# Making the low parts of the weights on VectorE instead of GpSimd in a decoder-layer kernel

## The reference

```python
h = rmsnorm(x, norm_pre_mix) * (1.0 + sc_m) + sh_m
proj = h @ w_in
(hq, hf, hi, hg, aq, ak, av, iq, ik, iw) = jnp.split(proj, split_points, axis=-1)
o_hg = hgrn2_mixer(hq, hf, hi, hg, ...)
o_att = dsa_mixer(aq, ak, av, iq, ik, iw, positions, ...)
y = jnp.concatenate([o_hg, o_att], axis=-1) @ w_out
x = x + gt_m * rmsnorm(y, norm_post_mix)
h = rmsnorm(x, norm_pre_ffn) * (1.0 + sc_f) + sh_f
gate, up = jnp.split(h @ w_ffn_in, 2, axis=-1)          # 1024 -> 2 x 2816
y = (jax.nn.silu(gate) * up) @ w_ffn_out                # 2816 -> 1024
x = x + gt_f * rmsnorm(y, norm_post_ffn)
```

## Time and profile before

| | us |
|---|---|
| median of 3 runs | 853.19 (852.34 to 853.39) |
| the profiled execution | 851.23 |
| its span | 849.4 |
| TensorE busy in it | 771.6 (91%) |
| VectorE / ScalarE / GpSimd busy | 326.3 / 284.0 / 278.2 |

### The profile page before, as it was taken

The page is one execution under the profiler, slowest core; times in us unless marked ns, Lnnn a source line. Parts: engine busy times, 40 slices in busy tenths (PEclk is TensorE's granted clock), DMA queues, the critical chain, the costliest instruction groups (busy, mean ns, idle before and its releaser), DMA issues.

```text
span 849.4 us, 10172 instructions
## 1 busy us (share of the span) xinstructions
PE 771.6 (91%) x3530; PEld 591.9 (70%) x3530; DVE 326.3 (38%) x651; ACT 284.0 (33%) x458; POOL 278.2 (33%) x156
## 2 busy tenths in 40 slices
PE   3697988999999887998997999999999996999996
PEld 2175655777776656665686788888888885888885
DVE  1198237969697762432405500000000003222214
ACT  4153344242423233324326522222222222122222
POOL 1154220313132122115540444444444445344430
PEclk9689899999999998998999899999999998999999
...
DMA packets 100594, 87.99 MB, mean 104 GB/s; under 512 B 3828, under 2 KB 89944, under 8 KB 99544
## 3 DMA queue, kind: packets, MB, share of 16 engines
...
...
## 4 chain that ended last, share of the span: by engine, by line
PE 76%; DVE 13%; issue 5%; ACT 2%; DMA 2%; SPq 1%; DVEq 0%; POOL 0%; ACTq 0%; POOLq 0%
PE ps L1131 43%; PE ps L1150 19%; PE ps L1307 2%; PE ps L1188 2%; DMA w_raw<-in_w_in 2%; DVE score L901 1%; DVE score L937 1%; PE ps L1375 1%; DVE act L966 1%; DVE top L932 1%; PE ps L1370 1%; PE ps L1350 1%; PE ps L1184 1%; PE ps L1434 1%; DVE h_lo L815 1%
## 5 line engine op out<-in xcount | busy, mean ns | idle before, releaser
L402 POOL TENSOR_TENSOR w_lo<-w_raw,w_hi 128x1024 fp32r<-128x1024 f32 (+1 forms) x107 | 255.6, 2399 | 532.9 <-ACT w_hi L461 532.9
L1131 PE MATMUL ps<-h_hi,w_hi 128*128 128x512 f32 x616 | 253.9, 412 | 9.1 <-DVE h_lo L815 6.5
L1131 PE MATMUL ps<-h_lo,w_hi 128*128 128x512 f32 x616 | 243.6, 395 | 0.0
L1131 PE MATMUL ps<-h_hi,w_lo 128*128 128x512 f32 x616 | 243.6, 395 | 0.0
L1131 PEld LDWEIGHTS ps<-h_hi,w_hi 128*128 128x128 f32 x616 | 117.6, 191 | 51.6 <-issue 18.4
L461 ACT ACTIVATE w_hi<-w_raw 128x1024 fp32r<-128x1024 f32 (+1 forms) x107 | 110.0, 1050 | 125.7 <-PE ps L1150 99.7
L1131 PEld LDWEIGHTS ps<-h_hi,w_lo 128*128 128x128 f32 x616 | 117.4, 191 | 26.2
L1131 PEld LDWEIGHTS ps<-h_lo,w_hi 128*128 128x128 f32 x616 | 117.8, 191 | 23.9 <-issue 1.2
L1150 PE MATMUL ps<-w_hi,h_hi 128*128 128x512 f32 x240 | 95.1, 396 | 7.2 <-DVE h_lo L1106 6.4
L1097 DVE TENSOR_TENSOR act<-adaw,ps 128x512 f32 x22 | 15.1, 688 | 221.9 <-PE ps L1131 221.9
L1150 PE MATMUL ps<-w_lo,h_hi 128*128 128x512 f32 x240 | 94.3, 393 | 0.0
...
## 6 DMA issues: line engine op xcount, KB each, us to landing
...
```

The costliest lines, as they stand in the source:

```text
L402: pool.tensor_tensor(w_lo[slot][:, 0:n], w_raw[slot][:, 0:n], w_hi[slot][:, 0:n].bitcast(f32), ALU.subtract).then_inc(lo_ok, 1)
L1131: last = mm(ps[bank][0:rows, :], a, b, start=(k == 0 and n == 0), stop=(k == KT - 1 and n == 2))
```

## The change

From group 25 on (the key projection of head 1) the low parts of the weights are made by VectorE: 82 of the 107 splits, and all eight `split_x_lo`. GpSimd ends after group 24. The splits are put into VectorE's order by hand: in a head one behind the ropes, one before the fourth reduction and one behind the last `normalise`; in the last head the activation splits ahead of the ropes and, with a weight split each, behind the first and second `normalise`; in FFN-in two before each of a pass's multiplications; in FFN-out one behind each `split_act`.

In the last FFN-in group TensorE now counts `h_free` after each of its first four steps, and VectorE splits `act` into slots 0 to 3 as they come free. TensorE starts FFN-out with row tiles 0, 2 and 3 of the first group and takes tile 1, whose banks hold the last multiplication's input, when `act_ok[1]` says so. The last pass of FFN-in is written out behind the loops of TensorE and VectorE.

```diff
@@ gpsimd
             with pool.Fori(0, HG_HEADS) as h:
                 stage_hg(h)
-            with pool.Fori(0, ATT_HEADS) as h:
-                stage_att(h)
...
-            with pool.Fori(0, FT // 2) as i:
-                for u in range(4):
-                    split_lo(i * 4 + (G_FIN + u), u)
-            with pool.Fori(0, FT // 4) as i:
-                for u in range(4):
-                    split_lo(i * 4 + (G_FOUT + u), u)
...
+            split_lo(G_ATT + 2, 2)
+            split_lo(G_ATT + 3, 0)
@@ vector
+            def split_lo(g, slot, n=1024):
+                ve.wait_ge(hi_ok, g + 1)
+                V.tensor_tensor(w_lo[slot][:, 0:n], w_raw[slot][:, 0:n], w_hi[slot][:, 0:n].bitcast(f32),
+                                ALU.subtract).then_inc(lo_ok, 1)
+            def split_x_lo(k):
+                ve.wait_ge(xs_hi, k + 1)
+                part_k = slice(k * SEQ, (k + 1) * SEQ)
+                V.tensor_tensor(h_lo[:, part_k], mix[:, part_k], h_hi[:, part_k].bitcast(f32),
+                                ALU.subtract).then_inc(xs_ok, 1)
...
             def att_body(h, first, last):
                 rot = slice(0, 32)
                 for n, dst in enumerate((aq, ak)):
+                    if last:
+                        split_x_lo(n)
                     ve.wait_ge(a_swap, h * 2 + (n + 1))
...
+                split_lo(h * 3 + (G_ATT + 4), 1)
                 if first:
                     head_tail(HG_HEADS - 1)
...
                     if t:
                         normalise(t - 1)
+                    if last and t in (1, 2):
+                        split_x_lo(t + 1)
+                        split_lo(G_OUT + 1 + t, 1 + t)
+                    elif not last and t == 2:
+                        split_lo(h * 3 + (G_ATT + 5), 2)
                 normalise(TT - 1)
+                if not last:
+                    split_lo(h * 3 + (G_ATT + 6), 0)
                 adaln_set(h)
...
+            for k in range(4, KT):
+                split_x_lo(k)
+            for k in range(4, KT):
+                split_lo(G_OUT + k, k % 4)
             ve.wait_ge(x_again, 16 * TT)
...
             ve.wait_ge(scale_ok, 2)
+            split_lo(G_FIN, 0)
             norm_features(1, 24, scale_ffn)
-            with ve.Fori(0, FT // 2) as i:
+            split_lo(G_FIN + 1, 1)
...
+            with ve.Fori(0, FT // 2 - 1) as i:
                 for v in range(2):
+                    for u in (2 * v + 2, 2 * v + 3):
+                        split_lo(i * 4 + (G_FIN + u), u % 4)
+                    swiglu(i, v)
...
             def split_act(k, slot):
                 at = slice(slot * SEQ, (slot + 1) * SEQ)
-                ve.wait_ge(group_done, k + (G_FOUT - 3))
+                if isinstance(k, int) and k < 4:
+                    ve.wait_ge(h_free, k + 1)
+                else:
+                    ve.wait_ge(group_done, k + (G_FOUT - 3))
...
+            for u in (2, 3):
+                split_lo(G_FOUT - 4 + u, u)
+            swiglu(FT // 2 - 1, 0)
+            ve.wait_ge(act_ok[0], 2)
+            ve.wait_ge(act_ok[1], 2)
+            split_lo(G_FOUT, 0)
+            for u in range(3):
+                split_act(u, u)
+            swiglu(FT // 2 - 1, 1)
+            split_lo(G_FOUT + 1, 1)
+            split_act(3, 3)
+            split_lo(G_FOUT + 2, 2)
+            split_lo(G_FOUT + 3, 3)
             for v in range(2):
                 ve.wait_ge(act_ok[v], FT // 2)
-            ve.wait_ge(group_done, G_FOUT)
-            with ve.Fori(0, FT // 4) as i:
+            with ve.Fori(1, FT // 4) as i:
                 for u in range(4):
                     split_act(i * 4 + u, u)
+                    split_lo(i * 4 + (G_FOUT + u), u)
@@ tensor
                 if k == KT - 1:
                     last.then_inc(group_done, 1)
+                elif freeing:
+                    last.then_inc(h_free, 1)
...
-            with te.Fori(1, FT // 2) as i:
+            with te.Fori(1, FT // 2 - 1) as i:
                 fin_pass(i, False)
-            for v in range(2):
-                te.wait_ge(act_ok[v], FT // 2)
-            for k in range(4):
-                row_group(G_FOUT + k, k, k, KT + k + 1, k == 0)
+            fin_pass(FT // 2 - 1, False, True)
+            te.wait_ge(lo_ok, G_FOUT + 1)
+            te.wait_ge(xs_ok, KT + 1)
+            te.wait_ge(act_ok[0], FT // 2)
+            for t in (0, 2, 3, 1):
+                if t == 1:
+                    te.wait_ge(act_ok[1], FT // 2)
+                last = row_tile(0, 0, t, True)
+            last.then_inc(group_done, 1)
+            for k in range(1, 4):
+                row_group(G_FOUT + k, k, k, KT + k + 1)
```

43 lines of the change are left out of this document (14 added, 29 removed).

## The result

The changed kernel takes 840.33 us, median of four runs (839.40 to 840.88), against 852.77 us (851.62 to 853.39, four runs) for the kernel before: a ratio of 0.9855, 95% interval 0.9838 to 0.9872. The profiled execution took 840.83 us, with a span of 838.9.

The account below looks back on a forecast made before the run. TensorE, busy 91% of the span, bounds the kernel, so only its waits can earn: -7.75 - 2.0 + 0.5 - 1.63 + 1.04 + 0.85 = -9.0 us, from 851.23 to 842.2, plus 2 for the median: 844.2 us, range 841.0 to 848.0.

Parts of the forecast that it names:

- Price of a split: VectorE's cost for one moved 128x1024 weight split: 1.25 us, extrapolated from 256 and 512 columns; bounds 0.75 and 2.4.
- rival (c): Moved splits cost VectorE the same 2.4 us as GpSimd: +8.7 us, 852.9 us, no change; chance 0.04.
- Step to FFN-out: From FFN-in to FFN-out: TensorE's 6.42 us gap and 1.33 us lost at half clock both go, -7.75 us.
- Rival (b): Handover to FFN-out only half covered: TensorE idles up to 2 us, half clock stays, 847.5 us; chance 0.1.
- Start of FFN-in: First FFN-in groups: subtractions no longer stretched by GpSimd, -2.0 us, between 1.3 (clock still drops) and 2.6.
- rival (a): Kinder clock: no half clock in the first head and at FFN-in, -1.3 and -0.6, 842.3 us; chance 0.2.
- Head 0 and the gates: First attention head +0.5 us, including +1.3 for half clock; gates behind it -1.63 us as their split moves.
- Heads 1 and 2: Split between ropes and first logits reduction delays TensorE's fourth logits by 0.52 us per head: +1.04 us.
- Last head: Activation split ahead of first rope delays the partner matmul; fillers wait 0.6 + 0.5 us for splits: about +0.85 us.
- The step that failed: From the forecast profiled execution, 842.2 us, to the median: 2 us added as before, giving 844.2 us.
- (d): FFN-in, pair of splits behind the third group: above 2.5 us each VectorE's queue delays TensorE, +16, 860 us; chance 0.03.
- (e): Change fails to do what it says, if TensorE frees no slot before its last matmul; counted under Rival (b).

Follow-up runs that it names:

- r1: Changed kernel with all its moved splits but the old step from FFN-in to FFN-out, without the slot-by-slot splitting: 845.84 us, ratio 0.9937.
- r2: Kernel before with only the slot-by-slot splitting and new row tile order; GpSimd still makes all low parts: 848.95 us, ratio 0.9969.
- r4: The changed kernel timed again, same code, in five rounds against the kernel before: 840.97 us, ratio 0.9883.
- r3: Changed kernel, but GpSimd keeps the splits up to the output projection (groups 0 to 40, eight activation splits): 841.59 us, ratio 0.9893.

## Why the prediction was short in its time, and how its terms fared

- **Price of a split**, 1.25 us: 1.22 measured. The extrapolation from half the size held; rival (c), 2.4 us on VectorE as on GpSimd, falls. The Trainium skill, "Perfetto Trace Analysis", section "Optimizing Scalar/DVE Operations", warns that offloading between GpSimd and VectorE might not help; here it did, with 1.22 us in place of 2.4 and no row of the FFN stretched any more. The prediction's 2.00 us beside a split, against 0.41, is this row of the kernel before:

```profile
284.91 2.00 DVE L964 TENSOR_TENSOR act<-act 128x256 f32<-128x256 f32 x1
```

- **Step to FFN-out**, -7.75: -7.97. The room everywhere was there, and r1 and r2 show that it needed both parts. Rival (b) did not occur: VectorE began slot 0 at 708.75 and TensorE never waited.
- **Start of FFN-in**, -2.0: -2.46. Mis-sized: I took the half clock to stay in part; it went altogether, in this as in r4's trace. The bound of 2.6 was the better value. That is the half of rival (a) that came true.
- **Head 0 and the gates**, -1.13: -1.03 in the first pair of traces, -1.6 on average. The first agreement is two misses that cancel: head 0 cost 0.97 where 0.5 was said, the gates gave 2.00 where 1.63 was. The wait of 2.4 us ahead of the third logits is 2.69. The gates' gap fell by 1.62 as said, and the products behind it took 5.44 us instead of 5.81, a gain that was put at nothing. The half clock in head 0 was put at +1.3 us as if it were certain. In six traces it was absent once, lasted 3.3 us four times (1.6 us lost against the trace without it) and 6.9 us once (3.0 us lost).
- **Heads 1 and 2**, +1.04: +0.67, 0.33 each instead of 0.52.
- **Last head**, +0.85: +1.44, +1.3 on average. One part of the mechanism was right: the partner matmul waits behind the activation split, 0.74 us longer where 0.6 was said. The other was wrong: the 0.6 + 0.5 us of idle charged for fillers that wait behind the queued splits came out at 0 in this trace and 0.3 in two others, and the wait of 0.79 us ahead of the logits went. TensorE idles no longer than before; the whole +1.44 is half clock, 10.0 us of it in this trace against 6.6 before, for which the forecast had no term here.
- **The step that failed** is the last one, from the profiled execution to the median: "the median of the runs, 853.19, lies 2 above it, so 844.2". What was wrong in it is the base: it took the 2.0 us between one execution and the median of three runs as a fixed distance that the changed kernel would have too. Those three runs lay 1.3 us above the median of 59, and the changed kernel's median lies 0.5 us below its own profiled execution. With the 1.2 us that its trace gained before any changed instruction (scatter: that stretch varies by 3.6 us over 13 traces of the same code), the result comes out as -9.3 - 1.2 - 2.0 - 0.5 = -13.0 against 853.19 (measured: -12.9). The forecast of the trace, 842.2, was 1.4 us from the profiled 840.83; the 2.0 put on top made it 3.4, and 3.9 from the median. And the range took in the unknown costs but not that executions of one kernel spread over 5.7 us.
- **Rivals (d) and (e).** No FFN wait appeared; (d)'s room of 2.5 us for a split was right to 0.3 for the first of a pair and wrong in counting both splits of a pair against one room.

What stays open: why nine runs of the changed kernel are 11.1 us below the 59 of before when the mean stretches give 10.0 (the last may be scatter: a single run of either spreads by 3 to 6 us), whether the heads are better left to GpSimd (r3), and what decides the clock behind a wait.
